# A recurrent stage written in rounds: projection halves and one convolution tap change rounds, and three weight splits are issued earlier

## The reference, cut to what matters

```python
h = modulate(rms_norm_3(x, g_norm1), shift1, scale1)
u = h @ w_in                                   # u_conv (2048), u_rwkv (3*1024 + 256), u_gate (2048)
y_conv = conformer_conv(u_conv, ...)           # za * sigmoid(zb), then a causal depthwise convolution of 31 taps
y_rwkv = rwkv7_mix(u_rwkv, ...)                # token shift, r, k, v, decay w, a; 16 heads of 64:
# per token: S = S*w + (S a) b^T + v k^T ;  y = S r ; then a group norm, a bonus and a gate
merged = g_conv * y_conv + g_rwkv * y_rwkv
x = x + gate1 * (merged @ w_out)
h2 = modulate(rms_norm_3(x, g_norm2), shift2, scale2)
x = x + gate2 * (square(relu(h2 @ w_ff1)) @ w_ff2)
```

## Time and profile before

| | |
|---|---|
| median of 3 runs | 3431.42 us (3430.13 to 3439.47) |
| the profiled execution | 3424.76 us |
| its span, first to last instruction | 3422.9 us |
| share of the span: PE busy | 93% |
| DVE, ACT, POOL busy | 57%, 39%, 11% |
| mean granted PE clock | 0.97 |
| matmuls, DVE, ACT, POOL instructions | 21690, 3488, 2204, 334 |

### The profile page before, as it was taken

The page is one execution under the profiler, slowest core; times in us unless marked ns, Lnnn a source line. Parts: engine busy times, 40 slices in busy tenths (PEclk is TensorE's granted clock), DMA queues, the critical chain, the costliest instruction groups (busy, mean ns, idle before and its releaser), DMA issues.

```text
span 3422.9 us, 52272 instructions
## 1 busy us (share of the span) xinstructions
PE 3189.9 (93%) x21690; PEld 2576.4 (75%) x21690; DVE 1963.2 (57%) x3488; ACT 1322.5 (39%) x2204; POOL 370.6 (11%) x334
## 2 busy tenths in 40 slices
PE   6898899999999899999999988889999989999998
PEld 5676778888787688887767765667777768778887
DVE  4545467764433577754466357487777754564444
ACT  2434233223323342223343236465655634333321
POOL 0001100000000000000000000154555510000000
PEclk9998999999999999999999999989989989999999
DMA  3220024442222134432311220211111103323321
GB/s 132 68 74 1 26 80 148 137 141 93 74 87 74 39 121 147 133 127 92 111 51 56 64 96 1 86 54 42 45 36 42 48 11 118 111 86 99 99 95 65
DMA packets 296298, 274.81 MB, mean 80 GB/s; under 512 B 9344, under 2 KB 284928, under 8 KB 295296
## 3 DMA queue, kind: packets, MB, share of 16 engines
q1 hardware_dynamic: 291808, 256.07, 23.2%
q10 hardware_dynamic: 4256, 15.40, 1.3%
HBM read 265.16 MB, written 6.29 MB: 79 GB/s over the span
## 4 chain that ended last, share of the span: by engine, by line
PE 81%; DVE 10%; ACT 5%; issue 2%; POOL 0%; DMA 0%; DVEq 0%; POOLq 0%; ACTq 0%; SPq 0%
PE ps L95 80%; DVE f L107 3%; DVE f L101 2%; DVE r L101 2%; PE ps L98 1%; ACT f L92 1%; ACT r L92 1%; ACT f L88 1%; DVE f L104 1%; ACT f L89 1%; ACT L88 1%; DVE f L110 1%; POOL f L101 0%; DVE f L3804 0%; DVE f L113 0%
## 5 line engine op out<-in xcount | busy, mean ns | idle before, releaser
L95 PE MATMUL ps<-r,r 128*128 128x512 f32 (+2 forms) x10344 | 2430.4, 394 | 85.9 <-DVE r L101 67.1
L95 PEld LDWEIGHTS ps<-r,r 128*128 128x128 f32 x10344 | 1916.5, 190 | 521.8 <-issue 89.9
L101 DVE TENSOR_TENSOR r<-f,r 128x1024 fp32r<-128x1024 f32 (+2 forms) x628 | 653.8, 1048 | 406.8 <-ACT r L92 401.8
L95 PE MATMUL ps<-f,f 64*64 64x64 f32 (+8 forms) x10430 | 716.8, 257 | 121.7 <-ACT f L92 42.6
L92 ACT ACTIVATE r<-f 128x1024 fp32r<-128x1024 f32 (+2 forms) x555 | 509.4, 929 | 739.9 <-PE ps L95 608.7
L95 PEld LDWEIGHTS ps<-f,f 64*64 64x64 f32 (+3 forms) x10430 | 591.4, 154 | 266.9 <-issue 92.2
L101 POOL TENSOR_TENSOR f<-f,f 128x512 f32<-128x512 f32 (+2 forms) x272 | 326.0, 1211 | 489.9 <-ACT f L88 234.8
L92 ACT ACTIVATE f<-ps 128x256 f32<-128x256 f32 (+4 forms) x448 | 188.6, 446 | 485.8 <-PE ps L95 372.5
L107 DVE SCALAR_TENSOR_TENSOR f<-f,f,f 128x128 f32<-128x128 f32 (+2 forms) x566 | 323.2, 573 | 46.7 <-ACT f L88 30.6
L101 DVE TENSOR_TENSOR f<-ps,f 128x512 f32<-128x512 f32 (+7 forms) x339 | 184.1, 554 | 280.3 <-PE ps L95 270.0
L88 ACT ACTIVATE f<-ps 128x512 f32<-128x512 f32 (+3 forms) x213 | 117.4, 557 | 563.8 <-PE ps L95 563.4
(11 more groups left out here) (35 smaller groups left out, 729.2 us busy)
## 6 DMA issues: line engine op xcount, KB each, us to landing
f<-in_w_mlp_up SPq DMA_DIRECT2D x32, 1024.0 KB, 6.0
f<-in_w_mlp_down SPq DMA_DIRECT2D x32, 1024.0 KB, 6.1
f<-in_w_ff SPq DMA_DIRECT2D x32, 1024.0 KB, 5.2
f<-in_w_in SPq DMA_DIRECT2D x26, 1024.0 KB, 5.0
f<-in_w_ada SPq DMA_DIRECT2D x48, 512.0 KB, 3.9
f<-in_w_in SPq DMA_DIRECT2D x40, 512.0 KB, 3.5
f<-in_w_in_odd SPq DMA_DIRECT2D x12, 1024.0 KB, 5.2
f<-in_w_in_even SPq DMA_DIRECT2D x11, 1024.0 KB, 5.1
```

The lines of the kernel that those rows point to most:

```text
L95: return self.e.matmul(out, l, r, start=first, stop=last)
L101: return self.e.tensor_tensor(out, a, b, op)
```

## The change

Three things change, and nothing is added to or taken from the work itself.

1. **Rounds.** In the rounds ahead of the first unit the six projection halves stand in k = 4, 5, 6, 7, 8, 9 (before: 4, 5, 6, 7, 10, 11). In all later rounds they stand in k = 4, 5, 6, 9, 10, 11, that is, the second half of the k projection goes from k = 7 to k = 9. Convolution tap 2 on DVE goes from k = 9 to k = 7.
2. **Norms.** A norm can carry a `lead`, the key of the first piece behind it. At n = 7 of the layer before, ACT calls `G.act(lead)` ahead of the last square, and DVE calls `G.dve(lead)` behind its part. The first piece is already split there by the rule "one beyond", so what this issues is the second piece's split. It is set for the norm ahead of `rw.x` and for the one ahead of `mlp3`.
3. **ACT at the entry.** `G.act(("cf.a", 0))` is issued ahead of the tanh and the sigmoid of the low-rank parts instead of behind them. It splits the piece of `cf.b` 0.

```diff
@@ Norm.__init__
-        self.K, self.gain, self.x_done, self.dst, self.shift = K, gain, x_done, dst, shift
+        self.K, self.gain, self.x_done, self.dst, self.shift, self.lead = K, gain, x_done, dst, shift, None
@@ ahead_act
             if kt == 7:
                 norm.table_act(act)
+                if norm.lead is not None:
+                    norm.K.G.act(act, norm.lead)
             if kt >= 0:
                 norm.square_act(act, kt)
@@ ahead_dve
         norm.square_dve(dve, n)
+        if n == 7 and norm.lead is not None:
+            norm.K.G.dve(dve, norm.lead)
@@ Conformer
-    ROUND_OF = (5, 6, 9, 10, 11, 11, 0, 0, 1, 3, 3, 4)
+    ROUND_OF = (5, 6, 7, 10, 11, 11, 0, 0, 1, 3, 3, 4)
@@ Rwkv
-    PROJ = (4, 5, 6, 7, 10, 11)
+    ENTRY, PROJ = (4, 5, 6, 7, 8, 9), (4, 5, 6, 9, 10, 11)
@@ Rwkv.steps
                 elif k in ("proj", "proj1"):
-                    if r < 84 and r % 12 in self.PROJ and (not split or r % 2 == (k == "proj1")):
+                    at = self.PROJ if r >= 0 else self.ENTRY
+                    if r < 84 and r % 12 in at and (not split or r % 2 == (k == "proj1")):
                         n = r // 12 + 1
-                        yield 2 * n, n, 0, "proj", self.PROJ.index(r % 12)
+                        yield 2 * n, n, 0, "proj", at.index(r % 12)
@@ Rwkv.act
         act.e.dma_start(K.spill["x_rest"], K.x).then_inc(S("d_spill"), 16)
+        G.act(act, ("cf.a", 0))
         act.wait_ge("rw_mix", 1)
@@ Third.__init__
-        self.X = self.norm.X
+        self.X, self.norm.lead = self.norm.X, ("rw.x", 0)
...
-        self.out.after = self.norm1
+        self.out.after, self.norm1.lead = self.norm1, ("mlp3", "up", 0, 0)
```

## The result

| | before | after |
|---|---|---|
| median of the runs | 3430.88 us (3417.66 to 3439.47, 13 runs) | 3441.77 us (3431.55 to 3452.22, 13 runs) |
| profiled execution, span | 3424.76, 3422.9 us | 3448.81, 3446.7 us |
| ratio of the runs | | 1.0034, 95% interval 1.0021 to 1.0046 |

A forecast was written before the change was run, and what follows sets the result against it. PE, busy for 93% of the span, was taken to bound the kernel. Terms -1.3 - 1.3 - 2.0 - 2.7 - 0.5 + 8 = +0.2 us gave 3425.0 profiled, 3431.5 for the median; range 3420 to 3443.

The forecast's parts named there:

- the bound of 0.3%: Whole kernel: 10.3 us taken as the least measurable change; chances 0.67 within it, 0.20 faster, 0.13 slower.
- the rival of the half at half clock: Moved 12 matmuls in k = 9 run at half clock in every pair: +3.0 us per pair, 3443; chance 0.14.
- Leads and the earlier `G.act`: PE's waits for weight splits vanish: -1.3 us ahead of `rw.x`, -1.3 ahead of `mlp3`, -2.0 ahead of `cf.b` 0.
- Entry: Before the first unit, PE's 7.24 us wait falls to about 1 but moves to `pB`: -2.7 us, bounds -5 and -1.
- First pair: k = 7 to 9: the moved half fills PE's 4.28 us hole ahead of k = 10; -0.5 us, bounds -3 and +1.
- that chain becomes 1.6 later: In the first pair, the half ahead of `pD` delays DVE's work leading to round 11 by 1.6 us.
- Steady rounds: Six later pairs: the half's move costs +1.3 us per pair, +8 in all; bounds -0.5 and +3.0 per pair.
- In k = 9 PE has no room: Steady k = 9: PE idles only 0.22 us before the last `ct`, so the 12 added matmuls cost about 4.2 us.
- the first rival: PE's clock returns as the half starts in k = 9, each steady pair near zero: 3421 to 3424; chance 0.22.
- the second rival: k = 9 is entered throttled and the moved half stays at half clock throughout: +3.0 us per pair, 3443; chance 0.14.
- is part of what eats the gains: Steady pairs: DVE's later token shift of the k projection, 0.75 us, stands ahead of the x phases and eats gains.
- The sign of being right: Steady pairs: new PE waits of about 2.5 us in k = 7, 1.5 to 2 in k = 8; 12-round windows 74 to 77.

The follow-up runs named there:

- experiment 1: The changed kernel with all rounds as before, leaving the two norm leads and the earlier `G.act`; 0.9985 of the kernel before, -5 us.
- Experiment 2: The kernel before with only the projection half moved to k = 9 and tap 2 to k = 7, from round 0 on; ratio 1.0053, +18 us.
- run 6: The changed kernel with ACT's two convolution products ahead of its two copies in k = 9; 0.9997 of the kernel before.
- run 7: The changed kernel with DVE's token shift of the k projection at the end of k = 10 instead of in k = 9; 1.001 of the kernel before.
- run 8: The changed kernel with ACT's products ahead of its copies in k = 9 and DVE's token shift behind `pE` in k = 10; 0.9955 of the kernel before.
- runs 10 and 12: Kernel before with only tap 2 moved to k = 7, 1.0008; changed kernel with ACT's and DVE's orders changed and tap 2 in k = 9, 0.9959 of before.

## Why the prediction came out as it did

The forecast time and the measured one are 10.3 us apart, inside the range near its upper end, and the ratio lies just past the bound of 0.3%, for which 0.13 had been given, with the bound inside its interval. That the time fell into the range is in part luck: the range's upper end, 3443, belonged to the rival of the half at half clock, which did not come. Step by step:

- **Leads and the earlier `G.act`: right.** -3.7 and -0.9 against -3.3 and -1.3; experiment 1 has -3.6 and -1.7.
- **Entry: right mechanism, size off.** The wait moved to `pB` as described, but -0.7 came out, not -2.7 (outside the bound of -1 as well). Three things make up the difference. DVE's six instructions, put at 1.52 us, took 1.66, 0.8 us more in all, since each lay beside an addition of POOL. v's shift started some 0.6 us later than the sum had it (2222.57 on the scale of before, not 2221.9). And `pA`'s instruction took 1.35 us instead of 0.35 beside POOL, 1.0 us that the sum had no term for.
- **First pair: wrong.** -0.5 was taken, between -3 and +1, and +3.1 measured. The half did fill PE's hole ahead of k = 10 (4.28 us), and rounds 7 to 10 took 19.15 us instead of 21.07. But "that chain becomes 1.6 later" was the term that decides, and it was too small: k = 11 took 10.35 us instead of 5.28. Experiment 2 shows that this comes from the steady move. Here the place of DVE's token shift is what counts most: rounds 7 to 11 take 28.56 us with only ACT's order changed (run 6) and 25.38 with only the shift's (run 7).
- **Steady rounds: near in size (+12.5 against +8), wrong in place.** The failed step is "In k = 9 PE has no room". It assumed a wait of 2.5 us in k = 7 (2.13 measured), one of 1.5 to 2 in k = 8 (none there), and a half that starts at the slow clock (4.2 us). Windows of after, from the end of the wait in k = 7 to the end of the half:

```profile
2494.17:2499.65 5.48, 5.30 (x85) 5.17 (x88) 5.42 (x10) 4.24 (x9) 5.34 (x5) 0.56 0.35 99
2499.65:2502.00 2.35, 2.35 (x39) 2.23 (x38) 2.00 (x5) 1.25 (x2) 2.06 (x3) 0.57 0.00 0
2502.00:2503.59 1.59, 1.59 (x49) 1.35 (x43) 1.56 (x4) 0.56 (x2) 1.45 (x2) 1.00 0.05 10
2503.59:2506.60 3.01, 3.01 (x16) 2.24 (x16) 0.84 (x3) 0.40 (x2) 1.66 (x2) 1.00 0.00 0
```

  PE worked on almost without a gap at the lower clock, mostly at 0.50 (1.2 GHz), and the clock was back at 1.00 (2.4 GHz) ahead of the half, which took 3.01 us. So the mechanism of the first rival was the true one for the clock, and k = 7 to 9 gained 1.1 us per pair (6.3 in six). Most of that gain is idle time and not the clock: in k = 7 to 9 of the six pairs PE is idle for 19.8 us before and for 14.4 after, since the new wait in k = 7 came in place of the one in k = 8 and not on top of it. The pair that was read the earlier trace rows is also one of those with little to gain: PE is idle for 2.50 us in its k = 7 to 9, and for up to 4.85 in the others.
  The rule that the prediction cites for the second rival from the Trainium skill ("TensorE: Matmul & The Clock Gate", Part 1), that the slow clock is the default and activity releases it, is not contradicted: the activity was `ct`'s, ahead of the half, and not the half's own.
- **What stood in its place was dismissed in one sentence**: that DVE's later shift "is part of what eats the gains", and that tap 2 gives nothing because DVE waits for `pD` anyway. The order behind PE's half was not followed through ACT and POOL. That costs 3.5 us per pair in k = 11 (21.1 in six). Run 6 takes 2.2 us per pair of it away, run 7 takes 2.1, and run 8, with both, 3.7: all of it.

The two errors had opposite signs: k = 7 to 9 was put at +1.3 us per pair and gave -1.1, k = 11 had no term and gave +3.5. So the sum came nearer than the reasoning. The sign of being right, windows of 12 rounds of 74 to 77 us, was met as well (77.00 and 76.52), for the wrong reason. That tap 2's move gives nothing was right (runs 10 and 12).

## What to carry to other kernels

When work is moved on PE, follow what waits for it on each other engine, and what stands behind that waiting instruction in the same queue: here two products behind two copies on ACT cost more than the move brought, and two changes of order turned +0.3% into -0.45%. A round that nothing was moved into can be the one that pays, so sum a profile by rounds before looking for the cause. And where an engine's instructions differ in length with what runs beside them, a delay of 0.7 us is not priced at 0.7 us: it may open or close an overlap that is worth more.

## What the runs showed of the hardware

DVE's instructions with two tensor operands in SBUF get much longer beside POOL's additions, and those with one of the two in PSUM do not. The answers for DVE's instructions of 128x512 by shape, rounds of the steady part (2300 to 2700 us), before, after, and kernel 8 (busy us, mean ns of one):

```profile
L101 DVE TENSOR_TENSOR f<-f,f 128x512 f32<-128x512 f32 x34 | 25.9, 761 | 0.4
L101 DVE TENSOR_TENSOR f<-f,ps 128x512 f32<-128x512 f32 x44 | 28.7, 671 | 0.0
```

```profile
L101 DVE TENSOR_TENSOR f<-f,f 128x512 f32<-128x512 f32 x30 | 30.1, 1004 | 0.3
L101 DVE TENSOR_TENSOR f<-f,ps 128x512 f32<-128x512 f32 x43 | 28.4, 673 | 1.6 <-PE ps L95 1.6
```

```profile
L101 DVE TENSOR_TENSOR f<-f,f 128x512 f32<-128x512 f32 x34 | 23.9, 702 | 0.4
```

The same instruction takes 761, 1004 and 702 ns in the three kernels. The form that reads its second operand from PSUM takes 671 and 673, though in the stage of after 32 of its 64 instructions lie beside an addition of POOL; none of the 64 took more than 0.69 us. Singly the form with both operands in SBUF took 0.68 or 0.69 us clear of POOL and 1.75 us when an addition had started 0.06 us earlier. This fits the Trainium skill, "SBUF — State Buffer", Who interferes with whom, by which VectorE and GpSimd share one pair of SBUF ports that only one of them can hold: a VectorE instruction with two SBUF inputs contends with a GpSimd instruction that reads SBUF, and one with at most one SBUF input does not, outside the modes that use two ports. The traces agree on both counts.

They also show the exception. `tensor_scalar`, which reads one tensor and which that section counts among those that can enter a two-port mode, gets longer beside POOL too: in the stages of before and after, its 128x256 form (`pA` on DVE) took 0.34 or 0.35 us in the 17 cases without an addition of POOL beside it, and 0.78 to 1.41 us in the 15 with one.

PE's clock: in after, rounds 57 to 59, the two waits of k = 11 (1.14 and 1.66 us) were followed by a fall to 0.50 and a round of 10.94 us, and in rounds 45 to 47 the same two waits (1.14 and 1.65) by none (9.46). The waits' lengths alone don't tell the two apart; what does was not settled.
